# Expert rows of v spread over the down pass, a later second gate tile, and sample sums behind the fifth turned chunk

## The chip, the cores and the metric

One Trainium2 chip, one core of it. The metric is the device time of one execution in microseconds (us); lower is better. Engines: PE is TensorE (matmuls; PEld its weight loads), DVE is VectorE, ACT is ScalarE, POOL is GpSimd, SP is SyncE, which here only issues DMAs. One megabyte (MB) below is a million bytes.

## The reference, cut to what matters

The kernel is one inference step of a decoder of two layers on 512 prompt tokens and 8 x 8 sample tokens, all float32. Layer 0 begins with a recurrent block, layer 1 with windowed attention. Each layer ends with the part that the change touches, a mixer that picks 16 of 16384 experts for each token and each of 8 heads:

```python
def chunk(args):                      # xc tokens, ec expert numbers, gc gates
    xc, ec, gc = args
    hc = jax.nn.gelu(jnp.einsum('chkd,cd->chk', u[ec], xc), approximate=False)
    return jnp.einsum('chk,chkd->cd', hc * gc, v[ec])
```

`u` and `v` are tables of 16384 rows of 1024 for each layer. A token's result is the sum over its 128 experts of gelu(u row . x) times gate times v row. After each layer comes an rmsnorm, which needs the mean of squares of each token.

## The kernel before

**Two ways of doing the experts.** Of 576 tokens, 384 (`DN`) are done densely: all 128 tiles of u (128 experts each) are multiplied with all 384 tokens in the *up pass*, the hidden values are multiplied with a gate matrix that is zero where an expert was not picked, and all 128 tiles of v are multiplied with them in the *down pass*. The other tokens (64 samples, 128 prompt tokens) are done sparsely: for each of 192 (`S0 + S1`) column positions POOL gathers 128 single rows (0.52 MB) by an indirect DMA, and DVE does one operation of 128x1024 with them. That is 192 gathers of u, then 192 of v, 384 in all (`GATH`), per layer. Below, one such gather of 128 rows is called a *row step*, numbered k from 0 to 383.

**The up pass** runs over m = 0..127. SP loads tile m (L449), ACT rounds it to the high part (`high_tile`, L758), POOL subtracts to get the low part (L600), PE does 24 matmuls of 384 columns (`up`, L1633), ACT writes gelu of the result (L800). Between, PE, ACT and DVE build the gates from one-hot rows (L1268, L1665, L777, L785) in groups of four tokens, and ACT stores them as 12 blocks of 2 MB to `gate_dram` (`store_gates`, L791). The hidden values of most tiles go to `s_dram`; those of the last eight (`KEPT`) stay, and the down pass begins with them (`turned_tile`).

**The down pass** runs over n = 0..127. SP loads tile n of v eight tiles ahead (`load_v`, L439), the hidden values in pairs (`load_hidden`, L435), and one tile of gates for each 8 steps (`load_gates`, L430, 1.57 MB, two slots). DVE multiplies hidden values and gates (`gate_hidden`, L1284), ACT rounds (`high_hidden`, L831, and `high_tile`), DVE takes the low parts (`low_hidden` L1289, `low_tile` L1297), PE does 18 matmuls of 512 columns (`down`, L1685).

**Row steps** are placed in DVE's order by `dots(n)`: n more of them (L1125 for u, L1132 for v). Before the down pass `DOTS_UP` of them are done, the last three behind the first low parts. In the down pass each n has one, and a second one where n is odd, until 384 are done. POOL's gathers are paced in the up pass by `gathers_by(m)`, whose last slope begins at m = `ROWS_V` and which ends at `DOTS_UP + 4`; after m = 127 POOL gathers as soon as a row slot is free. There are 8 slots (`ROWS`), so gather k waits for row step k - 8 to be done. Each engine runs its instructions strictly in the order written, and so does SP with its waits and DMA issues.

**At the end of the up pass** SP issues, in this order: v tiles 0 to 3 (`EARLY_V`) behind u tiles 123 to 126, the first gate tile once the last gate block is stored, v tile 4 once 125 up steps are done, the second gate tile, then v tiles 5, 6, 7, one more up step later each.

**After the down pass** (`residual`) the samples' two halves are folded (L1698), then for each of 8 chunks k PE turns four blocks into token-last layout (L1706), DVE adds them to the residual stream (L1357), ACT squares (L628), and PE sums the squares by matmuls with a matrix of 1/1024 (L1692). The squares of the samples (L625) are summed in L1711, behind chunk 0. Chunk k of 4 and above waits for the addition of chunk k - 4.

Of the kernel before, what the change touches and what calls it, by code (L numbers as in the profile page):

```python
# [38 lines left out]
KEYS = 128  # L39
# [9 lines left out]
GATH = 2 * (S0 + S1)  # L49
# [84 lines left out]
GE = 8  # L134
PHID0_AT, PHID1_AT = 64, 4
KEPT = 8
DOTS_UP = 214
ROWS_V, PACE_U = 118, 55
EARLY_V = (123, 124, 125, 126)


def turned_tile(n):
# [28 lines left out]
def gathers_by(m):  # L171
# [7 lines left out]
    else:  # L179
        n = min(72 + 1.99 * (m - PACE_U), S0 + S1 + 4)  # L180
    return min(int(n + max(0, 2.4 * (m - ROWS_V))), DOTS_UP + 4)

# [49 lines left out]
def decoder(nc, xin, consts, params, wts, wv, stconv, kcT, kc, vc, uT, u, v,  # L232
            yT, convP, hOut, kNew, vNewP, vNewS, kKeep, vKeep, convS, gate_dram, s_dram):
    with ExitStack() as ctx:
# [171 lines left out]
        @block.sync  # L406
        def _(spq):
            for h in range(2):
                spq.dma_start(xT[:, 4 * h:4 * h + 4], xin[:, 4 * h:4 * h + 4]).then_inc(sem(f"x_loaded{h}"), 16)
            spq.dma_start(prm[:, :], params).then_inc(sem("params_loaded"), 16)  # L410

            def load_weights(lo, hi):
                for w in range(lo, hi):
                    if W_OUT <= w < W_OUT + OUTS:
                        continue
                    if w == W_GATE[5]:
                        spq.wait_ge(sem("xc_used"), 1)
                        for f in range(OUTS):
                            spq.dma_start(outR[:, f], wts[W_OUT + f]).then_inc(sem("out_loaded"), 16)
                    if w - 2 in (W_A, W_X):  # L420
                        spq.wait_ge(sem("tile_done"), tiles_made(w - 2))
                    elif w >= 2:
                        spq.wait_ge(sem("w_split"), splits_made(w - 2 - OUTS * (0 <= w - W_OUT - OUTS < 2)))
                    spq.dma_start(raw[:, w % 2], wts[stored_at(w)]).then_inc(sem(f"w_loaded{w % 2}"), 16)

            def experts(l):
                w_end, d_end = (W_K, W_N)[l], (D_K, D_N)[l]

                def load_gates(g):
                    spq.dma_start(gt[:, g % 2], gate_dram[l].rearrange("b p (g n) -> p b g n", n=GE * GB)  # L430
                                  [:, :, turned_tile(g * GE) // GE]
                                  ).then_inc(sem(f"gt_loaded{g % 2}"), 16)

                def load_hidden(q):
                    spq.dma_start(sring[:, q % 4].rearrange("p a t -> p (a t)"), s_pairs[l, turned_tile(2 * q) // 2]  # L435
                                  ).then_inc(sem(f"s_loaded{q % 4}"), 16)

                def load_v(n):
                    spq.dma_start(tile_raw(KEYS + n), v_tiles[l, turned_tile(n)].rearrange("e (c d) -> e c d", c=NC)  # L439
                                  ).then_inc(sem(f"v_loaded{n % 8}"), 16)  # L440

                for m in range(KEYS):
                    if m < 2:
                        spq.wait_ge(sem("w_split"), splits_made(w_end - 2 + m))
                    elif m < 4:
                        spq.wait_ge(sem("tile_done"), d_end - 3 + m)
                    else:
                        spq.wait_ge(sem("mm_done"), after("mm_done", l, m - 3))
                    spq.dma_start(raw[:, m % 4], uT[l, m].rearrange("p (c e) -> p c e", c=NC)  # L449
                                  ).then_inc(sem(f"t_loaded{m % 4}"), 16)  # L450
                    if m in EARLY_V:
                        spq.wait_ge(sem("g_stored0"), after("g_stored", l, 16 * (NGB // 2)))
                        load_v(EARLY_V.index(m))

                spq.wait_ge(sem("g_stored0"), after("g_stored", l, 16 * (NGB // 2)))
                spq.wait_ge(sem("g_stored1"), after("g_stored", l, 16 * (NGB // 2)))
                load_gates(0)
                for q in range(4):
                    spq.wait_ge(sem("mm_done"), after("mm_done", l, KEYS - 3 + q))
                    load_v(q + 4)  # L460
                    if q == 0:
                        load_gates(1)
                for n in range(8, KEYS):
                    j = n - 8
                    spq.wait_ge(sem("mm_done"), after("mm_done", l, KEYS + j + 1))
                    load_v(n)
                    if j % 2 == 0:
                        if j < KEPT:
                            spq.wait_ge(sem(f"s_stored{j // 2}"), 16 * (l + 1) * (KEYS - KEPT) // 8)
                        spq.wait_ge(sem("h_split"), after("h_split", l, j + 2))  # L470
                        load_hidden(j // 2 + 4)
                    if j % GE == GE - 4 and j // GE + 2 < KEYS // GE:
                        spq.wait_ge(sem("h_mul"), after("h_mul", l, j + 4))
                        load_gates(j // GE + 2)

            load_weights(0, 3)
            spq.dma_start(cst[:, :], consts[:, 0:C_COS]).then_inc(sem("consts_loaded"), 16)
            load_weights(3, W_PQ0)

            load_weights(W_PQ0, W_K)  # L480
            spq.wait_ge(sem("state_kept"), 1)
            spq.dma_start(convP, keepP[:, :, :]).then_inc(sem("states_out"), 16)
            spq.dma_start(convS, keepS[:, :, :, :].rearrange("p c b k -> p (c b) k")
                          ).then_inc(sem("states_out"), 16)
            spq.wait_ge(sem("hlast_ready"), 1)
            spq.dma_start(hOut, hlast[:, :, :]).then_inc(sem("states_out"), 16)
            experts(0)
            for i in range(2):
                spq.wait_ge(sem("mm_done"), after("mm_done", 0, 2 * KEYS - 3 + i))
                load_weights(W_K + i, W_K + i + 1)  # L490
            spq.wait_ge(sem("row_used"), after("row_used", 0, GATH))
            spq.dma_start(atc[:, :], consts[:, C_COS:C_N]).then_inc(sem("atc_loaded"), 16)
            spq.wait_ge(sem("mm_done"), after("mm_done", 0, 2 * KEYS))
            spq.dma_start(wv_sb[:, :, :], wv).then_inc(sem("wv_loaded"), 16)
            load_weights(W_K + 2, W_Q + 2)

            spq.wait_ge(sem("v_ready"), 1)
            spq.dma_start(vNewP, vtok[:, NQB - 1]).then_inc(sem("out_done"), 16)
            spq.dma_start(vNewS, vtok[0:NB * TS, NQB]).then_inc(sem("out_done"), 16)
            spq.wait_ge(sem("k_ready"), 2)  # L500
            spq.dma_start(kNew, kR[:, :, TP - WIN:T]).then_inc(sem("out_done"), 16)
            load_weights(W_Q + 2, W_O + 2)
            spq.wait_ge(sem("tile_done"), D_O)
            for b in range(NB):
                spq.dma_start(vnew[:, b], vtok[b * TS:(b + 1) * TS, NQB]).then_inc(sem("vnew_loaded"), 16)
            spq.dma_start(kc_sb[:, :, :, :], kcT).then_inc(sem("kc_loaded"), 16)
            spq.dma_start(vc_sb[:, :, :], vc).then_inc(sem("vc_loaded"), 16)
            load_weights(W_O + 2, W_N)
            experts(1)
            for c in range(0, NC, 2):  # L510
                spq.wait_ge(sem("y_ready"), c + 2)
                spq.dma_start(yT[:, c:c + 2], xn[:, c:c + 2]).then_inc(sem("out_done"), 16)
            spq.wait_ge(sem("states_out"), 48)
            spq.wait_ge(sem("out_done"), 16 * (3 + NC // 2))
# [404 lines left out]
        def _(dve):  # L919
# [182 lines left out]
            def experts(l):  # L1102
                rows_done = 0
# [225 lines left out]
                for t in range(ND):  # L1329
                    one_hots(t)  # L1330
                dots(DOTS_UP - 3 - rows_done)
                for n in range(3):
# [5 lines left out]
                for n in range(KEYS):  # L1338
                    if n + 3 < KEYS:
                        gate_hidden(n + 3)  # L1340
                    dots(1)
                    if n + 2 < KEYS:
                        low_hidden(n + 2)
                        low_tile(KEYS + n + 2)
                    dots(n % 2)
                dots(GATH)

                dve.wait_ge(sem("mm_done"), after("mm_done", l, 2 * KEYS))
# [181 lines left out]
        def _(pe):  # L1530
# [72 lines left out]
            def experts(l):  # L1603
# [90 lines left out]
                def residual():  # L1694
# [6 lines left out]
                    for k in range(NC):  # L1701
# [3 lines left out]
                            src = ytok[:, c, k * P:(k + 1) * P] if c < ND else accS1[:, k * P:(k + 1) * P]  # L1705
                            ins = pe.transpose(ps[:, (2, 3, 0, 1)[k % 4], c * P:(c + 1) * P], src, ident)  # L1706
                        ins.then_inc(sem("y_turned"), 1)
                        if k == 0:
                            pe.wait_ge(sem("sq_ready"), SQ[2 * l + 2] + 1)
                            for c in range(NC):  # L1710
                                pe.matmul(ps[:, SUMS, 0:SMP], ones[:, :], xn[:, c, TP:T],  # L1711
                                          start=(c == 0), stop=(c == NC - 1))
# [242 lines left out]
```

## Time and profile before

| | |
|---|---|
| median of 3 runs | 3247.98 us (3240.16 to 3249.84) |
| the profiled execution | 3246.93 us, its span in the trace 3245.1 us |
| mean granted TensorE clock | 0.971 of full speed |
| busy: PE, DVE, POOL, ACT | 3072.5, 2547.9, 1815.1, 1383.9 us |
| moved by DMA | 920.92 MB, 284 GB/s over the span |

The order of time: layer 0's mixer has its up pass from 356 to 1000.6 us and its down pass from 1012.1 to 1559.7 us; layer 1's run from 2003 to 2652 us and from 2664.4 to 3209.1 us. The page's slices show PE busy for nine tenths nearly everywhere, and DMA at nine tenths through most of both passes. Busy PE time is not work at its peak, and an engine's share over the whole span does not say which wait ends last at a given place; for that the stretches around the end of the up pass, the middle of the down pass and the end of it are read separately.

### The profile page before, as it was taken

How to read it: one execution, taken by the hardware profiler on the slowest of the kernel's cores; microseconds unless marked ns; L12 is line 12 of the kernel's file. 1: busy time of each engine (PE TensorE's matmuls, PEld its weight loads, DVE VectorE, ACT ScalarE, POOL GpSimd, SP SyncE). 2: the span in 40 equal slices, each digit the busy share in tenths (PEclk: the TensorE clock that was granted, in tenths of full speed). 3: DMA queues.
4: the chain of work that ended last, by engine and by line, in shares of the span. 5: the costliest groups of instructions: out<-in, count | busy, mean ns of one | idle time of the engine just before them, and what ended most of it. 6: DMA issues, size and time to landing. Idle time of an engine off the chain costs nothing.

```text
span 3245.1 us, 46734 instructions
## 1 busy us (share of the span) xinstructions
PE 3072.5 (95%) x17222; PEld 2779.0 (86%) x17222; DVE 2547.9 (79%) x4953; ACT 1383.9 (43%) x2559; POOL 1815.1 (56%) x1160
## 2 busy tenths in 40 slices
PE   8889999999998999999888999999999989999997
PEld 7779999999996877777675789899999978877786
DVE  7755999977766999996468358999877759989984
ACT  2522334567762333333344233334776743333332
POOL 4543488877775456560130223788777755555640
PEclk9989999999998999999988899999999989999998
DMA  3212499999999999996130112899999999999991
GB/s 109 72 52 94 150 334 336 343 405 388 394 389 385 401 399 400 401 398 240 49 97 1 39 60 84 312 321 345 377 397 384 408 378 395 399 401 401 398 351 65
DMA packets 286579, 920.92 MB, mean 284 GB/s; under 512 B 27344, under 2 KB 77392, under 8 KB 282688
## 3 DMA queue, kind: packets, MB, share of 16 engines
q1 hardware_dynamic: 154336, 415.63, 35.2%
q0 software_dynamic: 111280, 404.77, 32.8%
q10 hardware_dynamic: 20736, 97.53, 7.4%
q8 instruction: 138, 2.26, 0.3%
q14 instruction: 89, 0.73, 0.1%
HBM read 817.34 MB, written 102.38 MB: 283 GB/s over the span
## 4 chain that ended last, share of the span: by engine, by line
PE 63%; DVE 23%; DMA 9%; issue 2%; POOL 2%; ACT 1%; SPq 0%; DVEq 0%; ACTq 0%; POOLq 0%
PE ps L1685 24%; PE ps L1633 18%; PE ps L1559 11%; DMA sring<-s_dram 5%; PE ps L1665 5%; DVE ps L1132 2%; DVE low L1297 1%; DMA gt<-gate_dram 1%; POOL low L600 1%; DVE rowsB L1125 1%; DVE rowsA L1125 1%; DMA rowsB<-u,pick 1%; DVE cand L1214 1%; DVE cand L1221 1%; DVE slot L1227 1%
## 5 line engine op out<-in xcount | busy, mean ns | idle before, releaser
L758 ACT ACTIVATE high<-raw 128x1024 fp32r<-128x1024 f32 x512 | 542.6, 1060 | 973.1 <-PE ps L1685 630.4
L1633 PE MATMUL ps<-xh,high 128*128 128x384 f32 x2048 | 700.9, 342 | 25.6 <-POOL low L600 25.5
L600 POOL TENSOR_TENSOR low<-raw,high 128x1024 fp32r<-128x1024 f32 x256 | 613.5, 2397 | 158.0 <-ACT high L758 154.3
L1633 PE MATMUL ps<-xh,low 128*128 128x384 f32 x2048 | 688.6, 336 | 0.0
L1633 PE MATMUL ps<-xl,high 128*128 128x384 f32 x2048 | 687.3, 336 | 0.0
L1685 PE MATMUL ps<-high,hh 128*128 128x512 f32 x1536 | 486.7, 397 | 34.9 <-DVE low L1297 34.9
L1685 PE MATMUL ps<-low,hh 128*128 128x512 f32 x1536 | 482.1, 395 | 0.0
L1685 PE MATMUL ps<-high,hl 128*128 128x512 f32 x1536 | 481.2, 394 | 0.0
L591 POOL DMA_INDIRECT rowsA<-v,pick x192 | 287.4, 1497 | 253.6 <-DVE ps L1132 244.4
L1633 PEld LDWEIGHTS ps<-xh,high 128*128 128x128 f32 x2048 | 387.1, 189 | 33.0 <-POOL low L600 32.3
L591 POOL DMA_INDIRECT rowsB<-v,pick x192 | 295.1, 1537 | 192.2 <-DVE ps L1132 175.4
L1633 PEld LDWEIGHTS ps<-xl,high 128*128 128x128 f32 x2048 | 387.1, 189 | 0.0
L1633 PEld LDWEIGHTS ps<-xh,low 128*128 128x128 f32 x2048 | 386.2, 189 | 0.0
L1685 PEld LDWEIGHTS ps<-high,hh 128*128 128x128 f32 x1536 | 287.9, 189 | 109.6 <-DVE low L1297 43.3
L1685 PEld LDWEIGHTS ps<-low,hh 128*128 128x128 f32 x1536 | 288.9, 188 | 71.0
L1685 PEld LDWEIGHTS ps<-high,hl 128*128 128x128 f32 x1536 | 289.2, 188 | 69.1
L1297 DVE TENSOR_TENSOR low<-raw,high 128x1024 fp32r<-128x1024 f32 x256 | 311.2, 1216 | 0.0
L1559 PE MATMUL ps<-xh,high 128*128 128x288 f32 x1152 | 256.7, 305 | 51.5 <-DVE xl L937 41.3
L576 POOL CAST high<-raw 128x1024 fp32r<-128x1024 f32 x40 | 45.6, 1140 | 398.5 <-PE ps L1559 300.0
L1125 DVE SCALAR_TENSOR_TENSOR rowsB<-rowsB,ps 128x1024 f32<-128x1024 f32 x192 | 230.7, 1213 | 47.6 <-DMA rowsB<-u,pick 47.2
L1132 DVE SCALAR_TENSOR_TENSOR ps<-rowsA,phid,ps 128x1024 f32<-128x1024 f32 x192 | 245.9, 1281 | 27.1 <-DMA rowsA<-v,pick 26.6
L1559 PE MATMUL ps<-xh,low 128*128 128x288 f32 x1152 | 251.8, 301 | 0.0
(279 smaller groups left out, 5210.9 us busy)
## 6 DMA issues: line engine op xcount, KB each, us to landing
raw<-uT SPq DMA_DIRECT2D x256, 512.0 KB, 7.2
raw<-v SPq DMA_DIRECT2D x256, 512.0 KB, 13.9
gate_dram<-gblk ACTq DMA_DIRECT2D x24, 2048.0 KB, 12.3
gt<-gate_dram SPq DMA_DIRECT2D x32, 1536.0 KB, 20.3
s_dram<-sring ACTq DMA_DIRECT2D x120, 384.0 KB, 7.1
sring<-s_dram SPq DMA_DIRECT2D x120, 384.0 KB, 14.5
raw<-wts SPq DMA_DIRECT2D x74, 512.0 KB, 3.6
rowsB<-u,pick POOLq DMA_INDIRECT x192, 8.5
```

The lines of the kernel that those rows point to most:

```text
L576: pool.tensor_copy(high[:, w % 2], raw[:, w % 2]).then_inc(sem("wh_ready"), 1)
L591: pool.indirect_dma_start(out=row_slot(k), out_offset=None, in_=u if k < S0 + S1 else v, in_offset=bass.IndirectOffsetOnAxis(ap=pick[:, c: ...
L600: pool.tensor_tensor(low[:, m % 4], raw[:, m % 4], high[:, (m + 2) % 3].bitcast(F32), ALU.subtract).then_inc(sem("lo_ready"), 1)
L758: act.activation(high[:, (m + 2) % 3], tile_raw(m), ACT.Copy).then_inc(sem("hi_ready"), 1)
L1125: dve.scalar_tensor_tensor(row, row, 1.0, wide(XS0 if k < S0 else XS1), ALU.mult, ALU.mult, accum_out=phid[:, c:c + 1]).then_inc(sem("row_ ...
L1132: dve.scalar_tensor_tensor(wide(ACC), row, phid[:, c:c + 1], wide(ACC), ALU.mult, ALU.add).then_inc(sem("row_used"), 1)
L1214: chain.did(dve.tensor_tensor(eq[a], cabf[:, a, 0:nh].unsqueeze(3).broadcast_to([P, nh, TOPK, TOPK]), iotaP[:, 0:TOPK].unsqueeze(1).unsque ...
L1297: dve.tensor_tensor(tile_low(m), tile_raw(m), high[:, (m + 2) % 3].bitcast(F32), ALU.subtract).then_inc(sem("vlo_ready"), 1)
L1559: ins = pe.matmul(ps[:, dbank(d) + h, 0:H2], m[:, c], x[:, c, h * H2:(h + 1) * H2], start=(c == 0 and j == 0), stop=(c == NC - 1 and j == 2))
L1633: ins = pe.matmul(ps[:, m % 2, 0:DN], w[:, c], x[:, c, 0:DN], start=(c == 0 and k == 0), stop=(c == NC - 1 and k == 2))
L1665: ins = pe.matmul(ps[:, 2 + g % 2, i * P:(i + 1) * P], hotB[:, k], hotA[:, k], start=True, stop=True)
L1685: ins = pe.matmul(ps[:, YC[c] + d, :], h[:, n % 3, c * P:(c + 1) * P], w[:, d * 512:(d + 1) * 512], start=(n == 0 and i == 0), stop=(n == ...
```

## The change

Four constants and the places of three things change.

- `DOTS_UP` goes from 214 to 202: 12 row steps of v fewer before the down pass (22 to 10). POOL's cap goes with it, from 218 to 206 gathers before the end of the up pass.
- In the down pass the 182 row steps left are spread evenly over the 128 steps (`rows_by`), where 170 were done in the first 113 or so.
- `ROWS_V` goes from 118 to 117: the last slope of the gathers' pace begins one up step earlier.
- SP issues the second gate tile behind v tile 7, that is after all 128 up steps, where it was behind v tile 4, after 125.
- PE sums the samples' squares behind chunk 4, where it was behind chunk 0.

```diff
-DOTS_UP = 214
-ROWS_V, PACE_U = 118, 55
+DOTS_UP = 202
+ROWS_V, PACE_U = 117, 55
 EARLY_V = (123, 124, 125, 126)
+
+
+def rows_by(n):
+
+    return DOTS_UP - (DOTS_UP - GATH) * (n + 1) // KEYS
@@
                     load_v(q + 4)
-                    if q == 0:
-                        load_gates(1)
+                load_gates(1)
                 for n in range(8, KEYS):
@@
                         low_tile(KEYS + n + 2)
-                    dots(n % 2)
+                    dots(rows_by(n) - rows_done)
                 dots(GATH)
@@
                         ins.then_inc(sem("y_turned"), 1)
-                        if k == 0:
+                        if k == 4:
                             pe.wait_ge(sem("sq_ready"), SQ[2 * l + 2] + 1)
                             for c in range(NC):
                                 pe.matmul(ps[:, SUMS, 0:SMP], ones[:, :], xn[:, c, TP:T],
```

## Rows read from the trace of the kernel before

**Rows 1.** The page: the chain that ended last, by line, share of the span.
```profile
PE ps L1685 24%; PE ps L1633 18%; PE ps L1559 11%; DMA sring<-s_dram 5%; PE ps L1665 5%; DVE ps L1132 2%; DVE low L1297 1%; DMA gt<-gate_dram 1%; POOL low L600 1%; DVE rowsB L1125 1%; DVE rowsA L1125 1%; DMA rowsB<-u,pick 1%; DVE cand L1214 1%; DVE cand L1221 1%; DVE slot L1227 1%
```

**Rows 2.** The chain, 955 to 1030 us: start us, us, what.
```profile
974.56 11.86 DMA gate_dram<-gblk
986.51 22.39 DMA gt<-gate_dram
1012.14 17.91 PE ps L1685 x64
```

**Rows 3.** PE's timeline at both pass changes; in brackets the idle time before.
```profile
987.23 0.44 PE L1633 MATMUL ps<-xh,high 128*128 128x384 f32 x1 [1.22 <-POOL low L600]
994.64 0.69 PE L1633 MATMUL ps<-xh,high 128*128 128x384 f32 x1 [2.98 <-POOL low L600]
1012.14 1.22 PE L1685 MATMUL ps<-high,hh 128*128 128x512 f32 x2 [11.58 <-DVE low L1297]
...
2664.39 1.22 PE L1685 MATMUL ps<-high,hh 128*128 128x512 f32 x2 [12.11 <-DVE low L1297]
```

**Rows 4.** ACT's timeline between layer 0's passes, first and last.
```profile
1000.60 0.49 ACT L800 ACTIVATE sring<-ps 128x384 f32<-128x384 f32 x1 [6.29 <-PE ps L1633]
...
1009.58 1.46 ACT L831 ACTIVATE hh<-sring 128x384 fp32r<-128x384 f32 x3 [7.55 <-DVE sring L1284]
```

**Rows 5.** SP's issues of gate tiles; POOL's gathers around the pass change.
```profile
986.51 0.39 SPq L430 DMA_DIRECT2D gt<-gate_dram  x1
...
992.52 1.47 SPq L430 DMA_DIRECT2D gt<-gate_dram  x1
969.38 0.96 POOL L591 DMA_INDIRECT rowsA<-v,pick  x1 [0.16 <-issue]
998.51 0.94 POOL L591 DMA_INDIRECT rowsB<-v,pick  x1 [0.30 <-issue]
1016.64 0.94 POOL L591 DMA_INDIRECT rowsB<-v,pick  x1 [17.19 <-DVE ps L1132]
```

**Rows 6.** Line L430: landing times of all 32 gate-tile loads.
```profile
DMA to landing us min/median/max: 12.3/20.3/25.1
```

**Rows 7.** Stretches: PE, PEld, DVE, ACT, POOL busy (xinstructions), PEclk (granted clock), DMA share, GB/s.
```profile
1010.00:1015.00 5.00, 2.85 (x7) 2.30 (x8) 4.90 (x8) 1.04 (x3) 0.00 (x0) 0.50 1.10 374
1015.00:1020.00 5.00, 5.00 (x17) 3.95 (x16) 4.89 (x6) 0.49 (x1) 2.75 (x3) 0.66 0.76 263
1100.00:1150.00 50.00, 50.00 (x216) 40.25 (x215) 46.41 (x56) 17.44 (x24) 20.89 (x18) 1.00 1.04 399
1500.00:1550.00 50.00, 50.00 (x217) 40.34 (x216) 27.81 (x38) 17.67 (x24) 0.00 (x0) 1.00 0.34 115
```

**Rows 8.** DMA view of 1100 to 1400 us: all bytes moved.
```profile
DMA packets 44244, 119.97 MB, mean 400 GB/s; under 512 B 3516, under 2 KB 17340, under 8 KB 44225
```

**Rows 9.** PE's waits in each layer's down pass: total us, times, longest us.
```profile
PE ps L1685 <- DVE low L1297: 18.3, 6, 11.6
...
PE ps L1685 <- DVE low L1297: 16.6, 5, 12.1
```

**Rows 10.** DVE: the page's group of v row steps (busy us, mean ns); its waits, 1050 to 1470 us.
```profile
L1132 DVE SCALAR_TENSOR_TENSOR ps<-rowsA,phid,ps 128x1024 f32<-128x1024 f32 x192 | 245.9, 1281 | 27.1 <-DMA rowsA<-v,pick 26.6
...
DVE sring L1284 <- DMA sring<-s_dram: 32.5, 9, 6.8
```

**Rows 11.** PE's timeline after layer 1's down pass: the samples' sums and the last sums.
```profile
3215.39 3.68 PE L1711 MATMUL ps<-xn,ones 128*128 128x64 f32 x16 [0.65 <-ACT xn L625]
3225.85 5.32 PE L1692 MATMUL ps<-xn,ones 128*128 128x512 f32 x12
```

**Rows 12.** Layer 0: the samples' sums; up tile 121's low part, its first matmul.
```profile
1565.66 2.00 PE L1711 MATMUL ps<-xn,ones 128*128 128x64 f32 x16 [1.06 <-ACT xn L625]
954.94 2.36 POOL L600 TENSOR_TENSOR low<-raw,high 128x1024 fp32r<-128x1024 f32 x1 [1.53 <-ACT high L758]
962.24 0.42 PE L1633 MATMUL ps<-xh,high 128*128 128x384 f32 x1
```

## The prediction

> **What bounds the kernel now.** Base: the profiled execution, 3246.93 us with a span of 3245.1 us, 1.05 us under the median of the runs (3247.98 us). I read the chain that ended last first: 42% of it is PE in the up and down passes (L1633, L1685), but 5% is the loading of hidden values from `s_dram` and 1% that of a gate tile [rows 1]. So PE sets the time, with holes made by DMA. Then the two places of holes.
>
> *Between the passes.* The chain shows the last gate block stored in 11.86 us, then the first gate tile loaded in 22.39 us, then DVE's three operations and the first down matmul at 1012.14 us [rows 2]. PE had ended the up pass when ACT could start its last gelu, at 1000.60 us [rows 4], and stood 11.58 us, 12.11 us in layer 1; in layer 0 it had also waited 1.22 and 2.98 us for the low parts of the last u tiles, which were landing late [rows 3]. All this time the DMA engines were full (share 1.10 at 374 GB/s even at 1010 to 1015 us, [rows 7]), and what they carried is in POOL's and SP's order: from 969.38 to 998.51 us POOL gathered without a long pause, and only 6.01 us behind the first gate tile SP issued the second [rows 5].
>
> *In the down pass.* PE's waits sum to 18.3 us in layer 0, of which 11.6 are the start, so 6.7 us lie inside; in layer 1, 16.6 - 12.1 = 4.5 us [rows 9]. DVE had waited for hidden values there, 32.5 us [rows 10]. The stretches say why: at 1100 to 1150 us the DMA share is 1.04, at 1500 to 1550 us, when the row steps are over, 0.34, and PE does 217 matmuls in 50 us, that is 50 / 217 x 18 = 4.147 us per down step [rows 7].
>
> **The change part by part.**
>
> *(a) 12 gathers fewer ahead of the down pass.* Each is 128 x 4096 bytes = 0.524 MB; 12 are 6.3 MB, and at the 400 GB/s of [rows 8] 15.7 us of all DMA engines. With the cap at 206, the last paced gather is the one that before stood about at 969.38 us (k = 205); what followed until 998.51 us, 13 gathers, shrinks to one [rows 5]. What is outstanding then drains by about 986 us, so the gate block's store stays near its 11.86 us, and I give nothing for it. The first gate tile, issued at 986.5 us, then has SP's own queue for company: u tile 127, v tiles 4 and 5. Its landing is bounded by the fastest of 32, 12.3 us, and by what it took here, 22.4 us [rows 2, 6]: between 998.8 and 1008.9 us. I take 12.3, the row with least gather traffic beside it. Then it is no longer what comes last. What is late next: PE's last up step, then ACT's gelu (0.49) and the rounding behind it (1.05), and from the start of the first `hh` (1009.58) to PE's start (1012.14) 2.56 us [rows 2, 4]. So the gap is 0.49 + 1.05 + 2.56 = 4.1 us, and a landing up to about 1001 us costs nothing. Gain 11.6 - 4.1 = 7.5 us and 12.1 - 4.1 = 8.0 us; bounds 0 and these.
>
> *(b) The last u tiles.* With the gathers gone from about 986 us, tile 127 lands somewhat earlier; tile 126 hardly. Of the waits of 1.22 + 2.98 us [rows 3] I take back 1.5 us per layer; bounds 0 and 4.2.
>
> *(c) The clock.* After the gap the granted clock is 0.50 at 1010 to 1015 us and 0.66 at 1015 to 1020 us, that is the 1.2 GHz level for about 6 us of work, and full after [rows 7]. That costs about 3 us of PE. The shorter gap may still end at the low level: I take 1 us back per layer; bounds 0 and 3.
>
> *(d) The down pass.* Per step DMA must bring a v tile (0.524 MB), half a pair of hidden tiles (0.197), an eighth of a gate tile (0.197) and 1.5 gathers (0.786): 1.704 MB in 4.147 us are 411 GB/s, where the trace gives 400 [rows 8]. The shortfall of 2.7% over some 470 us is 12.6 us; a lead of about 5 us built up at the start covers part, and 6.7 and 4.5 us appear as holes [rows 9]. With 182 / 128 = 1.42 gathers the demand is 1.663 MB, 401 GB/s. The shortfall is 0.3% or 1.5 us over the pass, within the lead. I leave 1 us of holes: gain 5.7 and 3.5 us. The other bound is a loss, the second rival. DVE has room: it was busy 46.41 of 50 us at 1.5 row steps per step and each is 1.28 us [rows 7, 10]; 0.08 fewer per step make it about 45.2. In the last 15 steps it now has row steps where it was busy 27.81 of 50 us [rows 7]: 50 / 4.147 = 12 steps x 1.42 x 1.28 = 22 us more, under 50, and the 46.41 at 1.5 row steps bound it from above. The last three row steps follow `low_tile(127)`, two steps ahead of PE's end (8 us against 3.8), so the copy of the accumulator doesn't wait.
>
> *(e) The second gate tile, later.* SP issues it after 128 up steps instead of 125, at about 999 us instead of 992.52 [rows 5], behind v tiles 5 to 7 and ahead of v tile 8 and the first hidden pair. It is first needed by `gate_hidden(8)` in down step 5. With PE starting at about 1003 us that stands behind `low_tile(6)`, hence behind down step 3: about 1003 + 4 x 4.15 + 2 (cold clock) = 1022 us, and PE has about one step, 4 us, in hand. From 999 us that leaves 23 to 27 us against landings of 12.3 to 25.1, median 20.3 [rows 6]. Behind a late one would queue DVE's row steps and low parts, and PE behind those. I take 0.5 us per layer; bounds 0 and 4. Its bytes leave the way of the first gate tile, which is counted in (a).
>
> *(f) `ROWS_V`.* Two gathers come earlier from up step 118 on. POOL then meets the eight-slot limit and low part 121, at 954.94 us before [rows 12], comes up to 3 us later; PE begins with it at 962.24 us, and it would be ready at about 954.94 + 2.36 + 3 = 960.3. Nothing; bounds 0 and 1.
>
> *(g) The samples' sums.* Behind chunk 0 PE stood 1.06 us (layer 0) and 0.65 us (layer 1) for ACT's squares [rows 11, 12]. Behind chunk 4 the squares are long there and chunks 1 to 4 cover the wait; the sums' own 2.00 and 3.68 us stay on PE. Chunk 5 waits for the addition of chunk 1, long done. Next is PE itself up to the last twelve pieces (5.32 us) [rows 11]. Gain 1.0 and 0.6 us; bounds 0 and 1.1, with 0.5 against it if the low clock falls otherwise.
>
> Sum: layer 0: 7.5 + 1.5 + 1 + 5.7 - 0.5 + 1.0 = 16.2 us; layer 1: 8.0 + 1.5 + 1 + 3.5 - 0.5 + 0.6 = 14.1 us. 3246.93 - 30.3 = **3216.6 us**. Upper bounds of all gains: (7.5 + 4.2 + 3 + 6.7 + 1.1) + (8.0 + 3.8 + 3 + 4.5 + 0.7) = 42.5 us, 3204 us.
>
> **Rivals.**
>
> *Half of the gap stays.* The first gate tile shares SP's queue with u and v tiles and comes 5 us later than I take it (about 1004 us), and the second one costs its 4 us. Of the 5 us, 2 cost nothing by (a), so each layer loses 3 + 3.5 us of the gain: 3216.6 + 13 = 3229.6 us. For it: landings of 20.3 us are the median even in the down pass [rows 6]. Against: there row gathers run beside all of them.
>
> *The down pass becomes DMA's.* Slower than before: 12 more row steps (6.3 MB) in a pass whose DMA is full leave it no easy last 15 steps to catch up. It decides at the delivered rate: before, the pass took 1559.7 - 1012.1 = 547.6 us. At R GB/s the new one takes 128 x 1663 / R - 5 us if DMA sets it; with the other gains (11.6 us per layer in mean, (d) left out) the whole is slower if that is over 559 us, so below R = 377. At 374 it is 564 us: 16.6 - 11.6 = 5 us lost per layer, 3257 us. For it: nothing is spare any more, and one stretch shows 374 [rows 7]. Against: the mean of 300 us is 400 [rows 8], and that stretch is one of small pieces.
>
> Here a rule speaks against the change. The trace delivers 400 GB/s from and to HBM for 300 us [rows 8]. The Trainium skill, DMA: Bandwidth & Descriptors, section "Where 436 GB/s comes from", holds that for HBM transfers about 358 GB/s per core bind. By it the pass would take 128 x 1663 / 358 - 5 = 590 us, 31 us lost per layer, some 3308 us; the trace disagrees, and I give it 0.01.
>
> *It moves nothing.* The first gate tile waits for something else, as the bytes ahead in its own queue, and the holes in the down pass come from uneven arrivals rather than from the sum of bytes. Then (b), (c), (g) and a little of (d) are left: about 3241 us.
>
> **How the numbers follow.** Forecast 0.62, half of the gap 0.19, nothing 0.11, DMA's pass 0.07, the page's limit 0.01. The two first are faster by over 0.3% (9.7 us, about what a measurement of this kernel can tell from no change), the third within it, the last two slower: 0.81, 0.11, 0.08. The range takes in the forecast's bounds and the first rival with 8 us above it: 3204 to 3238 us.
>
> **What would show it.** In the new profile: the first gate tile landing in 12 to 14 us; PE's gap between passes near 4 us; few or no waits of L1685 for L1297 inside the pass, and DMA share near 1 until its last steps; L1711 without idle time. It is wrong if DVE waits for `gt` a second time in step 5, if DVE's waits for `sring` grow, or if gathers stay late in the last 15 steps so that the copy of the accumulator waits.

## The result

The changed kernel takes 3201.52 us in the median of 4 runs (3195.23 to 3209.76), the kernel before 3246.34 us beside it (3240.16 to 3249.84): a ratio of 0.9866, 95% interval 0.9851 to 0.9880. That is 1.3% faster; the medians differ by 44.8 us. The forecast was 3216.6 us with 3204 to 3238: the direction and the main mechanisms were right, the size was not, and the time lies 2.5 us below the range. The profiled execution took 3202.49 us.

The changed kernel's page; line numbers are 4 or 5 higher than before. First the span and the chain by line, to be held against [rows 1].

```profile
span 3200.7 us, 46734 instructions
PE ps L1689 34%; PE ps L1637 22%; PE ps L1563 11%; PE ps L1669 5%; POOL low L604 2%; DMA raw<-uT 1%; PE ps L1811 1%; DVE xn L948 1%; DVE xl L941 1%; DVE cand L1218 1%; DVE cand L1225 1%; DVE slot L1231 1%; PE ps L1765 1%; PE ps L1800 1%; DVE rowsB L1129 1%
```

The loading of hidden values (5% before) and of a gate tile (1%) are no longer among the 15 largest shares, and PE's two expert lines went from 42% to 56%. The time is shorter and more of it is PE's work.

The chain of the changed kernel around layer 0's pass change (start us, us, what), against [rows 2]:

```profile
977.72 8.94 DMA raw<-uT
...
987.82 2.41 POOL low L604
990.27 4.45 PE ps L1637 x24
...
995.13 1.05 ACT high L762
996.18 0.42 ACT hh L835
996.62 0.45 DVE hl L1293
997.10 1.23 DVE low L1301
998.37 11.75 PE ps L1689 x43
```

In layer 0 no gate tile is in it: what joins the passes is the last u tile and then the short chain of ACT and DVE. In layer 1 the gate tile is still in the chain, and makes the gap half a microsecond longer (4.2 us):

```profile
2617.41 9.55 DMA gt<-gate_dram
```

Layer 0 is close to that too. DVE's own timeline shows the first gate product waiting for its tile since 962.6 us, and the tile there at 995.10 us:

```profile
995.10 1.50 DVE L1288 TENSOR_TENSOR sring<-sring,gt 128x384 f32<-128x384 f32 x3 [32.49 <-DMA gt<-gate_dram]
```

SP had issued it at 985.42 us: 9.7 us, where it was 22.4 us. DVE's 32 us of waiting look alarming, but all except the last 0.4 us lie ahead of the end of the up pass (994.7 us), when DVE's row steps are over and nobody waits for it.

Inside the down pass PE has no listed wait at all. Two stretches of 50 us of the changed kernel's down pass, columns as in [rows 7]; layer 0's passes began at 1012.1 us before and 998.4 us now:

```profile
1236.40:1286.40 50.00, 50.00 (x217) 40.39 (x216) 44.39 (x53) 17.68 (x24) 20.31 (x17) 1.00 1.03 401
1436.40:1486.40 50.00, 50.00 (x217) 40.41 (x216) 44.88 (x53) 17.59 (x25) 19.55 (x17) 1.00 1.03 402
```

and two of the kernel before, the second as far from the start of its pass:

```profile
1300.10:1350.10 50.00, 48.48 (x208) 38.52 (x207) 43.48 (x51) 16.50 (x23) 27.43 (x17) 1.00 1.03 401
...
1450.10:1500.10 50.00, 47.92 (x206) 38.13 (x205) 42.40 (x51) 16.42 (x22) 15.63 (x10) 1.00 0.97 364
```

The number to read is the count of matmuls (x217, x208, x206), not the busy time. In nine stretches of 50 us, from 38 us behind the start of the pass, the kernel before did 1913 in layer 0 and 1924 in layer 1, the changed one 1953 and 1954. A stretch's count takes in the matmuls that lie across its two edges, so 50 / 217 = 0.230 us is a little short for one; from start to start a matmul takes 0.232 us. The 40 and 30 missing matmuls are then 9.3 and 7.0 us; PE's waits listed 6.7 and 4.5 us for the same holes [rows 9].

The marks of both profiled executions, in us:

| | before, layer 0 / 1 | changed, layer 0 / 1 |
|---|---|---|
| last gate store to end of the up pass | 26.0 / 25.6 | 19.7 / 18.8 |
| end of the up pass to first down matmul | 11.6 / 12.1 | 3.7 / 4.2 |
| down pass | 547.5 / 544.7 | 536.9 / 536.8 |
| end of it to the root of the sums | 19.6 / 22.1 | 19.8 / 19.8 |

The first row has a weak point: the store itself moves. The first matmul of up tile 100 is a steadier mark. From there to the end of the up pass it is 153.7 and 153.3 us before, 147.8 and 149.0 us now, that is 5.9 and 4.3 us less.

### The profile page after: what moved, and what is told of

Same layout as the page of the kernel before. It is cut to its first block, busy times and chain, and to the rows that moved or that the text cites. A ratio compares the mean times of both kernels' runs of the same rounds, so it can differ in the third digit from the quotient of the medians.

```text
span 3200.7 us, 46734 instructions
## 1 busy us (share of the span) xinstructions
PE 3069.8 (96%) x17222; PEld 2780.8 (87%) x17222; DVE 2551.4 (80%) x4953; ACT 1382.4 (43%) x2559; POOL 1746.1 (55%) x1160
## 4 chain that ended last, share of the span: by engine, by line
PE 77%; DVE 16%; DMA 3%; POOL 2%; issue 1%; ACT 1%; DVEq 0%; ACTq 0%; SPq 0%
PE ps L1689 34%; PE ps L1637 22%; PE ps L1563 11%; PE ps L1669 5%; POOL low L604 2%; DMA raw<-uT 1%; PE ps L1811 1%; DVE xn L948 1%; DVE xl L941 1%; DVE cand L1218 1%; DVE cand L1225 1%; DVE slot L1231 1%; PE ps L1765 1%; PE ps L1800 1%; DVE rowsB L1129 1%
## 5 line engine op out<-in xcount | busy, mean ns | idle before, releaser
L595 POOL DMA_INDIRECT rowsA<-v,pick x192 | 271.3, 1413 | 296.9 <-DVE ps L1136 288.8
L1637 PEld LDWEIGHTS ps<-xh,high 128*128 128x128 f32 x2048 | 386.1, 189 | 20.8 <-POOL low L604 19.8
L595 POOL DMA_INDIRECT rowsB<-v,pick x192 | 240.2, 1251 | 271.0 <-DVE ps L1136 255.6
L1563 PE MATMUL ps<-xl,high 128*128 128x288 f32 x1152 | 252.5, 302 | 0.0
L1129 DVE SCALAR_TENSOR_TENSOR rowsA<-rowsA,ps 128x1024 f32<-128x1024 f32 x192 | 230.8, 1213 | 21.6 <-DMA rowsA<-u,pick 14.1
```

The costliest lines, as they stand in the source:

```text
L595: pool.indirect_dma_start(out=row_slot(k), out_offset=None, in_=u if k < S0 + S1 else v, in_offset=bass.IndirectOffsetOnAxis(ap=pick[:, c: ...
L1129: dve.scalar_tensor_tensor(row, row, 1.0, wide(XS0 if k < S0 else XS1), ALU.mult, ALU.mult, accum_out=phid[:, c:c + 1]).then_inc(sem("row_ ...
L1563: ins = pe.matmul(ps[:, dbank(d) + h, 0:H2], m[:, c], x[:, c, h * H2:(h + 1) * H2], start=(c == 0 and j == 0), stop=(c == NC - 1 and j == 2))
L1637: ins = pe.matmul(ps[:, m % 2, 0:DN], w[:, c], x[:, c, 0:DN], start=(c == 0 and k == 0), stop=(c == NC - 1 and k == 2))
```

## Experiments

All thirteen were compared with the kernel before on the same chip. "Marks" are the rows of the table above, read from each kernel's trace.

**1. Only the row steps.** The changed kernel with these two edits undone:

```diff
-                load_gates(1)
+                    if q == 0:
+                        load_gates(1)
@@
-                        if k == 4:
+                        if k == 0:
```

> The change with the second gate tile and the samples' sums left where they were before; only DOTS_UP, ROWS_V and the even spread. My theory (the gathers in front of the pass change and the sum of bytes in the down pass are the causes): the first gate tile lands in about 10 us instead of 22, since the second one stands behind it in SP's queue; PE's gap between the passes is about 4 us in both layers, no PE wait inside the down pass, about 3203 us. Rival (the second gate tile's bytes hold up the first): the first lands in 15 us or more, the gap stays 8 us or more, about 3215 us.

Measured: 3202.02 us median (3199.49 to 3205.83), ratio 0.9845 (0.9822 to 0.9867). Gap 3.7 us in both layers, down pass 536.7 and 537.8 us. DVE's first gate product began 8.8 and 9.1 us after the gate tile's issue, though the second gate tile was issued 1.3 us behind the first. The row steps alone carry the gain, except what the samples' sums give (experiment 5), which the medians can't show.

**2. Only the second gate tile.** The kernel before with this edit:

```diff
-                    if q == 0:
-                        load_gates(1)
+                load_gates(1)
```

> The kernel before with only the second gate tile issued behind v tile 7. My theory: gathers still fill the DMA engines, the first gate tile still needs 19 us or more, the gap stays at 9 us or more, the down pass keeps its holes; within 5 us of before, about 3244 us. Rival (the second gate tile holds up the first): the first lands in 14 us or less and the gap falls to 4 to 6 us in both layers, about 3231 us.

Measured: 3246.94 us median (3236.99 to 3256.47), ratio 0.9992 (0.9975 to 1.0009). Its chain between the passes:

```profile
979.64 12.08 DMA gate_dram<-gblk
...
991.81 22.51 DMA gt<-gate_dram
```

Moved away, the second tile left the first at 22.5 us. The gap stayed 11.9 and 11.2 us. This part of the change has no effect that can be seen, in either direction: in no trace of before, the changed kernel, 1 and 2 does DVE wait for a gate tile a second time. The Trainium skill, DMA: Bandwidth & Descriptors, section "Issuing engines are not separate DMA queues", says that transfers issued by several engines run on the same 16 DMA engines and interleave; experiments 1 and 2 agree, since a load on SP's queue was slow beside POOL's gathers (22.5 us, against 8.8 to 9.1 us with 12 gathers fewer) and not from its neighbour in its own queue.

**3. Fewer ahead, old pace.** The changed kernel with 1.5 row steps per down step:

```diff
-                    dots(rows_by(n) - rows_done)
+                    dots(n % 2)
```

> The changed kernel, but with 1.5 row steps per down step as before (one, and a second where n is odd), so that 182 end at about step 121. My theory (bytes): the pass change is as in the changed kernel, but the demand is 411 GB/s again for 121 steps, and each down pass gets 6 to 10 us longer by holes, about 3201.5 + 16 = 3218 us. Rival (the holes came from the state in which the pass starts, not from the pace): holes under 2 us per layer, about 3203 us.

Measured: 3216.55 us median (3214.58 to 3222.36), ratio 0.9888 (0.9867 to 0.9909). Gap 3.9 and 3.7 us, down pass 548.5 and 547.6 us, 1904 and 1912 matmuls in the nine stretches.

**4. Even spread, as many ahead as before.**

```diff
-DOTS_UP = 202
-ROWS_V, PACE_U = 117, 55
+DOTS_UP = 214
+ROWS_V, PACE_U = 118, 55
```

> The changed kernel with DOTS_UP back at 214 and ROWS_V at 118, so that 170 row steps are spread evenly over the down pass (1.33 per step, 389 GB/s). My theory: no holes in the down pass (it lasts about 537 us in each layer, from 547.5 and 544.7), but the gap between the passes stays at 9 us or more, since 12 more gathers stand ahead of it: about 3246 - 18 = 3228 us. Rival (the gap comes from the second gate tile): the gap falls to 4 to 6 us, about 3212 us.

Measured: 3227.05 us median (3225.93 to 3229.66), ratio 0.9923 (0.9902 to 0.9944). Gap 12.6 and 12.0 us, gate tile 22.5 us, down pass 536.9 us in both layers, DMA at 376 to 402 GB/s in its stretches. Experiments 3 and 4 take the change apart: with fewer row steps ahead but the old pace 33.0 us are gained, with the even spread but as many ahead 22.5 us. Neither is quite alone: both kernels also have the later second gate tile and the samples' sums behind chunk 4, which experiment 1 has not, so the sum of the two (55.5 us) counts the sums twice, and that it is above experiment 1's 47.5 us is not to be read. The marks are cleaner. From the last gate store to the first down matmul, experiment 3 takes 23.6 and 23.5 us and experiment 4 takes 38.0 in both, about as the kernel before (37.6 and 37.7); in the down pass experiment 4 gains what the change gains, and experiment 3 nothing.

Experiments 4 and 8 (below) differ in `DOTS_UP` alone, 214 and 202: with it the gate tile goes from 22.6 us to 9.6 and 11.0 us and the gap from 12.6 and 12.0 us to 3.7 and 4.3. Of all pairs this one shows most plainly that the gathers held the tile up. Whether by their bytes or by the number of their pieces, no run tells apart.

**5. Only the samples' sums.** The kernel before with `k == 0` made `k == 4`, run once.

> The kernel before with only the samples' sums moved behind chunk 4. My theory: the idle time ahead of the samples' sums (1.06 and 0.65 us) is gone and nothing else; the time from the end of each down pass to the root of the sums (19.6 and 22.1 us before) falls by about 1 us. Rival (it is paid back by TensorE's clock, since the short matmuls now keep PE at work in another order): it changes by up to 2 us either way with the stretch that runs at the low clock, and the changed kernel's 19.85 and 19.77 us come from that, not from the idle time. The whole within 0.3% of before.

Measured: 3243.35 us in one run, beside 3251.57 us. From the end of the pass to the root of the sums: 18.3 and 19.9 us. With the marks of all profiled runs: three kernels with the sums behind chunk 0 (before, 1, 2) show 19.6, 22.1, 23.5, 22.1, 22.1, 23.7, mean 22.2 us; the twelve profiled runs with them behind chunk 4 show 18.3 to 19.9, mean 19.4 us. So it is 2.8 us per layer, over three times the idle time, though the medians of experiment 1 and the changed kernel cannot show it.

The rival has the larger part. The mean granted clock over the 20 us behind each down pass was 0.91, 0.74, 0.66, 0.74, 0.74 and 0.66 behind chunk 0, in the order above, and 0.83 or 0.91 in all 24 cases behind chunk 4. At the same 0.91 the times are 19.6 and 18.3 us, so about 1.3 us come without the clock; the rest goes with it. Layer 1's sums in experiment 1 and in the changed kernel are the same 16 matmuls:

```profile
3173.15 3.68 PE L1716 MATMUL ps<-xn,ones 128*128 128x64 f32 x16 [0.65 <-ACT xn L630]
```

```profile
3176.64 1.90 PE L1715 MATMUL ps<-xn,ones 128*128 128x64 f32 x16
```

Experiment 1's granted clock was 0.50 in the 5 us around its sums, the changed kernel's had come back to full when it reached them. Why the low clock ends sooner in the new order is not shown.

**6. More DVE work, no byte more.** The changed kernel with, behind the row steps of each down step:

```diff
+                    if n % 2 == 0:
+                        chain.settle()
+                        chain.did(dve.tensor_tensor(slotT[:, 0], slotT[:, 1], slotT[:, 2], ALU.add))
```

> The changed kernel with one more DVE operation of 128x384 (about 0.47 us) in every second down step: no byte more, but more DVE time per step than 1.5 row steps would cost (1.42 x 1.28 + 0.24 against 1.5 x 1.28 + 0). Its result is not used. My theory (the holes in the down pass come from DMA bytes): no holes, the pass stays at 537 us in both layers, about 3202 us. Rival (the holes come from DVE being nearly full at 1.5 row steps): the pass grows to 543 us or more in each layer, about 3218 us.

Measured: 3202.90 us median (3195.66 to 3207.07), ratio 0.9845 (0.9821 to 0.9869). Down pass 537.9 and 536.9 us, 1954 and 1953 matmuls. A stretch of it:

```profile
1100.00:1150.00 50.00, 50.00 (x217) 40.30 (x216) 48.63 (x59) 17.50 (x24) 17.90 (x17) 1.00 1.04 397
```

DVE is busy 48.63 of 50 us, in the mean of layer 0's nine stretches 48.66, where the kernel before had 45.27, and PE loses nothing.

**7. More bytes, no DVE work more.** The changed kernel with, in SP's loop over v tiles 8 to 127 (a wait of ACT's in layer 1 keeps the tile free):

```diff
+                    if j % 14 == 4:
+                        x = 9 * l + j // 14
+                        if x:
+                            spq.wait_ge(sem("extra"), 16 * x)
+                        spq.dma_start(slotT[:, :, :].rearrange("p a n -> p (a n)")[:, 0:D], v_tiles[l, j]
+                                      ).then_inc(sem("extra"), 16)
```

> The changed kernel with one more load of 0.524 MB every 14 down steps, 9 per layer, into a tile that nothing reads: 4.7 MB more per layer, no DVE work more; the demand rises from 401 to about 410 GB/s. My theory: 4.7 MB are 11.8 us at 400 GB/s, of which 2 to 5 us are covered by the lead of the pass, so each down pass grows by 7 to 10 us to about 546 us with DVE waiting for hidden values, about 3218 us. Rival (DVE's load, not bytes): the pass stays at 537 us, 3202 us.

Measured: 3220.48 us median (3215.57 to 3225.17), ratio 0.9901 (0.9878 to 0.9924). Down pass 548.1 and 546.6 us, 1903 and 1916 matmuls. DVE's wait for hidden values between 1040 and 1500 us, this kernel (total us, times, longest us) and then the changed one:

```profile
DVE sring L1297 <- DMA sring<-s_dram: 45.7, 18, 6.8
```

```profile
DVE sring L1288 <- DMA sring<-s_dram: 18.4, 13, 2.4
```

That is 17.6 us above experiment 6, which was measured beside it, for 18 loads of 0.524 MB: 0.98 us each. The down passes by themselves are 11.2 and 9.8 us longer than the changed kernel's, 1.17 us for each load, against 1.31 us that one takes at 400 GB/s. Experiments 6 and 7 settle the holes: bytes, not DVE. And as the changed kernel stands at the brink, bytes in its down pass cost nearly their full price.

**8. The gathers' last slope one step later.** `ROWS_V` 118 in the changed kernel.

> The changed kernel with ROWS_V back at 118: the gathers' last slope begins one up step later. The last paced gather is then issued about 4 us later and drains later. My theory: the last u tiles land up to 2 us later, the up pass ends at about 995 to 997 us instead of 994.7, the first gate tile up to 2 us later, and all in all 0 to 3 us per layer, 3202 to 3208 us. Rival (the gathers' start, not their number, made the tail short): 5 us or more per layer, 3212 us or more.

Measured: 3203.86 us median (3196.22 to 3207.59), ratio 0.9850 (0.9824 to 0.9877). Last gate store to end of the up pass 21.8 and 21.6 us against 19.7 and 18.8. Counted from up tile 100, where the store's own shifts drop out, it is 149.0 and 149.3 us, against 147.4 to 149.3 us, mean 148.1, in the six profiled runs that share this part of the changed kernel (it, 1, 3, 6, 7 and 13). So `ROWS_V` is worth about 1 us per layer, at the edge of what the traces can tell, and the medians cannot.

**9 and 10. The number ahead.** The changed kernel with `DOTS_UP` 196, and with 208.

> The changed kernel with DOTS_UP 196: 188 row steps in the down pass, 1.47 per step. Theory of bytes: the demand is 0.918 + 1.47 x 0.524 = 1.688 MB per 4.147 us = 407 GB/s, 1.75% over the 400 delivered, 9.3 us over 531 us, less the 2 to 4 us of lead that the kernels with 1.5 row steps and with extra loads showed: each down pass grows from 537 to about 543 us; the gap between the passes stays 3.7 us, since ACT's and DVE's chain behind the last up step sets it. About 3202 + 12 = 3214 us. Rival (there is slack in the down pass as long as row steps end with it, and fewer in the tail is always as good): 3202 us or below.

> The changed kernel with DOTS_UP 208: 176 row steps in the down pass (395 GB/s), six more gathers ahead of it. From the last gate store to the first down matmul it was 23.4 us at 202 and 37.5 us at 214, that is 1.17 us per gather, near the 1.31 us that 0.524 MB take at 400 GB/s. Theory of bytes: 30.5 us here, the gap about 8 to 9 us, the down pass still 537 us: 7 us more per layer, about 3216 us. Rival (a threshold, as the second gate tile or the clock): either the gap stays under 5 us (3203 us) or it is back at 11 us (3226 us).

Measured: 196: 3206.28 us median (3198.37 to 3212.78), ratio 0.9852 (0.9812 to 0.9891), gap 3.7 us, down pass 542.0 and 541.6 us. 208: 3210.61 us (3205.12 to 3216.82), ratio 0.9868 (0.9829 to 0.9906), gap 3.7 us, down pass 536.9 us. At 196 the pass grew by 5 us, where 6 were expected, but the medians lie 4.8 us above the changed kernel and not 12, which their scatter doesn't separate. At 208 the gap was not 8 to 9 us: the delay moved ahead of it. Its chain:

```profile
979.69 12.92 DMA raw<-uT
...
996.17 5.96 PE ps L1637 x24
```

The last u tile took 12.9 us instead of 8.9, and the last up tile 5.96 us instead of 4.45. From the last gate store to the first down matmul it is 23.4 us at 202, 28.9 at 208 and 38.0 at 214 (experiment 4, with `ROWS_V` 118) in layer 0: no threshold.

**11. The last slope two steps earlier.** `ROWS_V` 115 in the changed kernel.

> The changed kernel with ROWS_V 115: the last slope of the gathers begins two up steps earlier. From 118 to 117 the time from the last gate store to the end of the up pass fell from 21.6 to 19.3 us. My theory: the gathers come still earlier, but the first eight v row steps wait for DVE's one-hot rows to end (the slots are full), POOL stands in front of them, and low parts of u tiles come late behind it; so nothing is gained, 3200 to 3206 us, with PE waits for POOL in the up pass of 0 to 3 us per layer. Rival (the tail still has DMA bytes to lose): the last gate block is stored 1 us sooner and 2 us per layer are gained, 3197 us.

Measured: 3225.54 us median (3217.17 to 3227.59), ratio 0.9914 (0.9888 to 0.9939): neither theory, but 24 us above the changed kernel, and 15 to 19 us above experiments 9 and 10 beside it. The waits in its trace between 940 and 990 us:

```profile
POOL rowsB L595 <- DVE ps L1132: 10.0, 1, 10.0
...
PE ps L1637 <- POOL low L604: 11.3, 2, 9.2
```

POOL issued eight v gathers while DVE was still at its one-hot rows, found all eight slots full, and stood 10.0 us in front of the ninth; behind it in POOL's order waited the low part of the next u tile, and PE stood 9.2 us for that. In the changed kernel the same wait is 2.8 us and reaches nobody. Layer 1 has the same wait of 9.2 us. I had named this mechanism and put 0 to 3 us on it. From up tile 100 to the end of the up pass it is 163.4 and 159.3 us, against the mean of 148.1 us: 15 and 11 us.

**12 and 13. A gap without the last up step in it, and the changed kernel again.** Experiment 12 lets the first down step depend on the gate tile alone:

```diff
+                    if m == KEYS - 1:
+                        high_hidden(l, 0)
+                        high_hidden(l, 1)
                     act.wait_ge(sem("mm_done"), after("mm_done", l, m + 1))
@@
+                for n in range(2):
+                    low_tile(KEYS + n)
                 for n in range(3):
                     gate_hidden(n)
                 for n in range(2):
                     low_hidden(n)
-                    low_tile(KEYS + n)
```

> The changed kernel in which the first down step no longer waits for the end of the up pass: DVE takes the low parts of v tiles 0 and 1 ahead of the first gate products, and ACT rounds hidden tiles 0 and 1 ahead of the last gelu. The first down matmul then waits only for the first gate tile's landing plus a gate product, a rounding and a low part (about 1.5 us). Theory: the tile lands about when the up pass ends, so the gap falls from 3.7 to about 1.5 us, and if the low clock comes from the gap the granted clock stays full at the start of the down pass and this takes 2 us less (535 instead of 537): 4 us per layer, 8 us in all against the changed kernel, about 3193 us. Rival (the clock falls anyhow, the gap alone counts): 2 us per layer, 3197 us.

> The changed kernel again, beside e12 on one chip. Both theories: 3198 to 3205 us, gap 3.7 to 4.2 us, down pass 537 us in both layers, last gate store to end of the up pass 19 to 20 us, end of the pass to the root of the sums 18 to 20 us.

Measured over 5 rounds on one chip: 12: 3194.09 us median (3189.79 to 3198.92), ratio 0.9826 (0.9807 to 0.9844); 13: 3199.78 us (3197.05 to 3214.11), ratio 0.9852 (0.9827 to 0.9876). The intervals overlap, and the marks give only a little: the gap was 3.5 and 3.1 us, not 1.5, since the gate tile now came last (DVE waited for it until 995.87 us, the up pass ended at 994.5); from the last gate store to the first down matmul 23.2 and 23.3 us against 23.7 and 23.8. So 0.5 us per layer are seen, not 4. The start stayed cold; this is experiment 12 from its first down matmul on:

```profile
997.90:1002.90 5.00, 4.97 (x15) 3.96 (x16) 4.79 (x6) 1.29 (x2) 2.24 (x3) 0.66 1.07 373
```

Whether its median is really below the changed kernel's stays open; of all kernels it has the lowest.

## Why the prediction was short

The steps that failed are (b), (d) and (g), terms with the right cause and too small a size: together 13.8 us in the forecast and some 31 us by the two profiled runs. Step by step, for layers 0 and 1:

| step | expected | in the profile |
|---|---|---|
| (a) the gap | 7.5 / 8.0 | 7.9 / 7.9 |
| (b) the last u tiles | 1.5 / 1.5, at most 4.2 / 3.8 | 6.3 / 6.8; from up tile 100 on 5.9 / 4.3 |
| (c) the clock at the start of the down pass | 1 / 1 | 1.4 / 1.4 |
| (d) holes in the down pass | 5.7 / 3.5, at most 6.7 / 4.5 | 9.3 / 7.0 |
| (e) the later gate tile | -0.5 / -0.5 | 0 |
| (g) the samples' sums | 1.0 / 0.6 | -0.2 / 2.3; over all runs 2.8 |

(c) is from the first 38 us of each down pass, 151 and 152 matmuls before, 157 and 158 in the changed kernel: 6 x 0.232 us. The right column, with (b) from the store and (g) of these two traces, sums to 50.1 us; the spans differ by 44.4. Of the rest, 0.6 us is the counting in whole matmuls, 0.4 us lie ahead of layer 0's last gate store and 4.7 us between layer 0's sums and layer 1's last gate store (1047.4 us before, 1052.1 us in the changed kernel), a stretch that measured 1043.3 to 1053.5 us over the runs without experiment 11. The change touches little of it, but 2.5 us of the 4.7 are layer 1's store coming later behind up tile 100, which is why (b) is smaller from there.

**(a) was right**, its mechanism too: the gathers held the gate tile up (4 against 8), and ACT's and DVE's chain of 4 us came next. The landing of 12.3 us that I took as the lower bound was too high: DVE began on the tile 9.7 us after its issue, and over that time the DMA engines moved only 280 GB/s. That the gap still has the expected length is partly luck, two errors that met: the up pass ended some 6 us sooner, and with that a landing of 12.3 us would have come late by about 3 us. At 9.6 us it was late by half a microsecond in layer 1.

**(b) was mis-sized, and its bound too.** I took the listed waits of 1.22 + 2.98 us [rows 3] as all there was to gain, and only 1.5 of them as likely. But the last up tile also ran at a low clock behind those waits: it began at 994.64 us and ended at 1000.5 us, 5.9 us where a tile takes 4.18, and that goes too when the waits go. And the tiles came earlier than "hardly": the waits of 4.2 us in layer 0 went to none, those of 3.8 us in layer 1 to 1.3. With 12 gathers fewer and `ROWS_V` at 117 the last paced gather was issued at 965.64 us, and DMA was no longer full from 980 us on (369 GB/s and 177 GB/s in the next two stretches of 5 us, 405 and 412 before). Of this `ROWS_V`, which (f) put at nothing, has about 1 us per layer (experiment 8); the rest comes from the number of gathers.

**(c) came out near its number, and by luck.** It rests on a shorter gap leaving less of the low clock, and the other traces don't bear that out. Over the first 5 us of the down pass the granted clock was 0.50 in both layers of the kernel before, but 0.63 and 0.55 in experiment 2 and 0.66 and 0.67 in experiment 4, with gaps as long. Behind the 22 short gaps (3.1 to 4.6 us) it was 0.50 in six, 0.66 to 0.71 in fifteen and full in one, experiment 9's layer 0 with a gap of 3.7 us:

```profile
996.60:1001.60 5.00, 5.00 (x22) 4.07 (x23) 4.78 (x5) 0.47 (x1) 1.54 (x2) 1.00 1.00 321
```

In the mean over all traces the first 38 us hold 155.1 matmuls behind the eight long gaps and 156.0 behind the short ones, a difference of 0.2 us. The 1.4 us of the table are what the two profiled runs happened to show.

**(d) had the right cause and a wrong size.** The sum of bytes (411 against 400 GB/s, 12.6 us less a lead of 5) gave 7.6 us; I then let the listed waits overrule it. The wait list counts a hole from the modelled end of the last matmul, and a matmul of 0.39 us is shown where one starts each 0.23 us; behind a hole three more matmuls stand 0.33 to 0.39 us apart, at full clock. So the list loses some 0.5 us at each hole; the count of matmuls gave 9.3 and 7.0 us. The sum itself had two errors that nearly cancelled. A down step is 18 x 0.232 = 4.18 us and not 4.147, so the demand was 408 GB/s before and is 398 in the changed kernel, where I had 411 and 401: the shortfall over 470 us was 1.9% or 9 us, not 12.6. And the lead is not 5 us: with 9 us of shortfall, 9.3 and 7.0 us of holes leave it 0 to 2 us. The other runs agree. Experiment 9's demand is 404 GB/s, 1.0% over 400, or 5 us in the pass; it grew by 5.1 and 4.8 us. Experiment 7's nine loads are 11.8 us; it grew by 11.2 and 9.8 us.

**(e)** The later gate tile cost nothing, as experiments 1 and 2 show together. **(g)** was sized by the idle time alone and left out the clock behind it: 2.8 us per layer over all traces, where 1.0 and 0.6 were expected. In the two profiled runs layer 0 shows none of it, since the kernel before had its highest clock of all (0.91) behind that pass.

**The rivals.** "Half of the gap stays" and "it moves nothing" fell with the first profile. "The down pass becomes DMA's" fell too, but narrowly: DMA moved 397 to 402 GB/s in full stretches, which is the demand of 398 and close to the 400 at which it fell short before, and experiment 7 shows that nine more loads bring all of the holes back. The Trainium skill's 358 GB/s for transfers with HBM (DMA: Bandwidth & Descriptors, "Where 436 GB/s comes from") is not borne out on this single core: the changed kernel moved 400 GB/s over layer 0's nine stretches, and its pass took 537 us, where the prediction's estimate from that figure was 590.

## What to carry to other kernels

Where DMA is full, work out the bytes per step of each phase against the rate that the trace delivers and move optional transfers until no phase is above it: 1.9% above gave 9.3 and 7.0 us in some 500, 1.0% gave 5, and 0.5% below gave none. Take the length of a step from start to start, since an error of 1% there is as large as what is looked for. Count finished matmuls per stretch to size holes; a list of waits gives a lower bound, and a low clock behind a wait has to be added where the rows show one. And before pulling transfers forward, look at what stands behind them in the issuing engine's order: one step earlier gained about 1 us per layer, two more lost 15 and 11.

## What the runs showed of the hardware

The same 1.57 MB load with pieces of 1 KB took 22.4 us beside the row gathers and was there 8.8 to 9.7 us after its issue in the changed kernel and experiment 1, where one gather was issued beside it. In the first case the DMA engines moved 397 GB/s: of the 8.9 MB moved meanwhile, the tile had 18%. I had not expected it below the 12.3 us that was the fastest of 32 loads before.

Behind a PE gap of 3.1 to 4.6 us the down pass began in 21 of 22 cases partly or wholly at the 1.2 GHz level (granted clock 0.50 to 0.71 over its first 5 us), and behind gaps of 11.2 to 14.2 us in all eight (0.50 to 0.67): how long the gap was made 0.2 us in the mean. The Trainium skill, TensorE: Matmul & The Clock Gate, Part 1, says that the throttled state is the default and activity releases it; the rows agree in that the clock came to full within 7 us of work in all of them. Shortening a gap from 12 to 3.5 us did not avoid the low start.
